# A head's groups of small matmuls moved earlier in the steps, to the places where attention's small matmuls stand

## The reference

```python
h = rmsnorm(x, w_norm_pre)
q_a, k_a, v_a, z_a, q_r, f_r, i_r, z_r = split(h @ w_in)
# attention: 8 heads of 64, 2 key heads, chunks of 64, a window of 2 chunks
s = einsum('bclhgd,bcmhd->bchglm', qc, kb) * scale
p = softmax(concat([s, sink]))[..., :-1]
o_a = einsum('bchglm,bcmhd->bclhgd', p, vb) * silu(z_a)
# recurrence: 4 heads of 128
f = lb + (1 - lb) * sigmoid(f_r);  G = cumsum(log(f)) in a chunk
A = causal(einsum('bclhk,bcmhk->bchlm', q*exp(G), k*exp(-G)))
o_intra = A @ v;  U = k_to_end^T @ v;  state = decay * state + U
o_inter = (q*exp(G)) @ state_before
o_r = rmsnorm(o_intra + o_inter) * silu(z_r)
x = x + rmsnorm(concat([o_a, o_r]) @ w_out, w_norm_post)
```

## Time and profile before

| | |
|---|---|
| median of 3 runs | 920.6 us (919.56 to 921.97) |
| the profiled execution's own time | 921.76 us |
| its span, first to last instruction | 920.0 us |
| TensorE matmuls busy | 904.5 us, 98% of the span |
| VectorE busy | 537.3 us, 58% |
| ScalarE busy | 426.4 us, 46% |
| GpSimd busy | 176.8 us, 19% |
| large matmuls (L424 and L433), count | 3 x 832 and 3 x 256 |

### The profile page before, as it was taken

One profiled execution on the slowest core, in us unless ns is written; L12 is line 12 of the kernel. 1 busy time (PEld: TensorE's weight loads), 2 busy tenths in 40 slices (PEclk: granted clock), 3 DMA queues, 4 the chain that ended last, 5 costly groups with the idle time before them and its releaser, 6 DMA issues.

```text
span 920.0 us, 12100 instructions
## 1 busy us (share of the span) xinstructions
PE 904.5 (98%) x4504; PEld 745.2 (81%) x4504; DVE 537.3 (58%) x959; ACT 426.4 (46%) x818; POOL 176.8 (19%) x138
## 2 busy tenths in 40 slices
PE   7998999999999999999999999999999999999997
PEld 6786878878888787888888878888888888788886
DVE  6758887784654765664254567555525366744523
ACT  7655366664444444454234534464423453444322
POOL 1001222520200203342020112243101011203102
PEclk9999999999999999999999999999999999999999
DMA  8785565738967543443785652354378553244463
GB/s 303 234 307 172 202 201 162 278 138 344 399 212 295 191 161 112 163 164 134 270 301 206 229 183 95 138 180 162 129 281 321 184 181 127 103 138 175 146 230 137
DMA packets 52636, 186.02 MB, mean 202 GB/s; under 512 B 5857, under 2 KB 6113, under 8 KB 52577
## 3 DMA queue, kind: packets, MB, share of 16 engines
q1 hardware_dynamic: 49840, 178.29, 54.2%
q10 hardware_dynamic: 2736, 6.95, 1.9%
HBM read 141.18 MB, written 44.04 MB: 201 GB/s over the span
## 4 chain that ended last, share of the span: by engine, by line
PE 87%; DVE 5%; ACT 4%; issue 2%; POOL 1%; DMA 1%; SPq 0%; DVEq 0%; ACTq 0%
PE bank L424 54%; PE bank L433 19%; PE bank L448 3%; PE bank L464 2%; PE bank L458 1%; PE bank L485 1%; PE bank L499 1%; PE bank L489 1%; PE bank L497 1%; PE bank L478 1%; DMA x_in<-in_x 1%; ACT w_hi L624 1%; PE bank L473 1%; DVE w_lo L825 1%; DVE f_c L1044 0%
## 5 line engine op out<-in xcount | busy, mean ns | idle before, releaser
L424 PE MATMUL bank<-h_hi,w_hi 128*128 128x512 f32 x832 | 331.4, 399 | 2.2 <-issue 1.1
L424 PE MATMUL bank<-h_hi,w_lo 128*128 128x512 f32 x832 | 329.5, 396 | 0.0
L424 PE MATMUL bank<-h_lo,w_hi 128*128 128x512 f32 x832 | 326.8, 393 | 0.0
L424 PEld LDWEIGHTS bank<-h_hi,w_hi 128*128 128x128 f32 x832 | 156.8, 188 | 47.8 <-issue 15.2
L424 PEld LDWEIGHTS bank<-h_lo,w_hi 128*128 128x128 f32 x832 | 157.0, 189 | 31.7 <-issue 0.2
L424 PEld LDWEIGHTS bank<-h_hi,w_lo 128*128 128x128 f32 x832 | 157.2, 189 | 30.2 <-issue 0.7
L1086 POOL TENSOR_TENSOR probs<-probs,s_stats 128x512 f32<-128x512 f32 x32 | 37.1, 1158 | 407.2 <-DVE s_stats L956 407.2
L433 PE MATMUL bank<-w_lo,mix_hi 128*128 128x512 f32 x256 | 100.0, 390 | 0.0
L433 PE MATMUL bank<-w_hi,mix_lo 128*128 128x512 f32 x256 | 99.9, 390 | 0.0
L433 PE MATMUL bank<-w_hi,mix_hi 128*128 128x512 f32 x256 | 99.6, 389 | 0.0
L825 DVE TENSOR_TENSOR w_lo<-w_raw,w_hi 128x1024 fp32r<-128x1024 f32 x37 | 49.7, 1352 | 23.3 <-ACT w_hi L624 23.2
(11 more groups left out here) (139 smaller groups left out, 1283.7 us busy)
## 6 DMA issues: line engine op xcount, KB each, us to landing
w_hi<-kept_hi SPq DMA_DIRECT2D x96, 512.0 KB, 3.7
w_lo<-kept_lo SPq DMA_DIRECT2D x96, 512.0 KB, 4.6
w_raw<-in_weights SPq DMA_DIRECT2D x40, 512.0 KB, 5.4
kept_hi<-w_hi SPq DMA_DIRECT2D x34, 512.0 KB, 5.9
kept_lo<-w_lo SPq DMA_DIRECT2D x34, 512.0 KB, 7.0
x_in<-in_x_rows SPq DMA_DIRECT2D x8, 1024.0 KB, 7.5
x_in<-in_x SPq DMA_DIRECT2D x15, 512.0 KB, 6.6
out<-q_gate ACTq DMA_DIRECT2D x9, 512.0 KB, 8.1
```

What stands on the lines that cost most here:

```text
L424: mm = pe.matmul(acc(w)[:, :], stationary[:, s, k, :], moving[:, k, :], start=(m == 0), stop=(m == 3 * KT - 1), skip_group_check=True)
```

## The change

Three numbers in `between` are other: the head's turns stand before large matmul 12 of their step instead of 18, its products before 4 instead of 8, its outputs before 4 instead of 10.

```diff
                 for h in range(HEADS):
-                    if w == gate(h) and m == 18:
+                    if w == gate(h) and m == 12:
                         head_turn(t, h)
-                    if w == gate(h) + 1 and m == 8:
+                    if w == gate(h) + 1 and m == 4:
                         head_products(t, h)
-                    if w == gate(h) + 2 and m == 10:
+                    if w == gate(h) + 2 and m == 4:
                         head_out(t, h)
                     if w == gate(h) + 3 and m == 18:
                         head_sum(t, h)
```

## The result

| | before | changed |
|---|---|---|
| median | 921.17 us (6 runs) | 924.45 us (6 runs, 922.50 to 926.78) |
| ratio, 95% interval | | 1.0036 (1.0022 to 1.0050) |
| span of the profiled execution | 920.0 us | 924.9 us |

What follows compares the result with a forecast made beforehand. TensorE bounds the kernel, its matmuls filling 904.5 of 920.0 us. Terms 0 (standing together) + 1.7 (tile 0) + 0.0 (head 3 later) + 0.1 (head 2's outputs) = +1.8 us on a 920.6 median: 922.4 us, range 920.4 to 924.4.

Steps and rivals of the forecast that it cites:

- Standing together: 16 moved groups that come to stand beside an attention group: no cheaper than apart, 0 us saved.
- Head 1's and head 2's turns, tile 0: L478 would wait for `v_r`, losing 0.65 us at head 1 and 0.73 us at head 2.
- Head 3's turns, tile 0: TensorE late by 1.37 us plus any later arrival of `v_r`, whatever was lost before: 1.7 us when tile 0 ends.
- the shift of `v_r`: Head 3, tile 0: how much later `v_r` comes, taken as +0.3 us, between about -0.5 and +1.38.
- The outputs of head 2: Tiles 1 and 2: wait for the last state of 0 to 0.1 us, taken as 0.1 for both together.
- the relief: Head 2, tile 1: earlier turns let GpSimd's L1109 and L1116 end near 395.8 and 397.1, states ready near 399.95.
- A wait before L497: Sign that the prediction is wrong; it expected L497 in tile 1 without a wait, or one under 0.1 us.
- the bounds: Limits on TensorE's lateness when tile 0 ends: 0.9 and 2.75 us.
- A: Head 2's and head 3's inputs stay: 2.75 us in tile 0, 0.74 in tiles 1 and 2 each; 924.8 us; chance 0.15.
- B: Groups standing together save 1.4 us against 1.8 lost: +0.4, 921.0 us; chance 0.1.
- C: Tile 0 catches up: `v_r` of head 3 comes 0.5 us earlier, tile 0 costs 0.9, 921.5 us; chance 0.2.
- D: Both B and C, and attention's wait for ScalarE shrinks by at most 0.7 us: -1.2, 919.4 us; chance 0.05.

Runs made afterwards that it cites:

- Experiment 4: Kernel before, with the turns, products and outputs at the changed places in tiles 1 to 3 only; ratio to the kernel before 0.9992.
- experiment 8: Changed kernel, with the squares of the next tile's x at other steps, taking one GpSimd add from ahead of L1116; ratio to the kernel before 1.0043.
- experiment 5: Changed kernel, with head 3's turns in tile 0 back before large matmul 18; ratio to the kernel before 1.0012.
- experiment 1: Kernel before, with only the heads' turns moved, before large matmul 12 instead of 18 in all tiles; ratio to the kernel before 1.0040.
- experiment 6: Kernel before, with only head 3's turns in tile 0 moved, before large matmul 12 instead of 18; ratio to the kernel before 1.0018.
- experiment 10: Kernel before, with only head 3's turns in tile 0 moved later, before large matmul 23 instead of 18; ratio to the kernel before 0.9984.
- experiment 11: Kernel before, with head 3's turns before 23 and the first chunk's weighted values before 21 instead of 12, both in tile 0; ratio 0.9980.
- experiment 12: Kernel before, with head 3's turns before 23 and the first three chunks' weighted values before 21, in tile 0; ratio 0.9964, 917.96 us.
- experiment 7: Changed kernel, with ScalarE's and GpSimd's split of attention's outputs (L772, L1109) one step earlier; ratio to the kernel before 1.0095.

## Why the prediction was wrong, point by point

*Standing together: 0.* Right. Experiment 4 has 12 merged groups, and over them its trace keeps the distances of before to 0.05 us. In the changed kernel turns and weighted values together cost 1.66 us in tiles 1 to 3, which is 0.88 + 0.78. TensorEngine Tiling (Array Packing), Key Properties, in the Trainium skill says that it is the change of mode that drains; the trace agrees.

*Head 1's and head 2's turns, tile 0: 0.65 and 0.73.* Right: 0.68 and 0.80 by the lateness. But attention's wait in step 16 gave 0.3 back ahead of them, and the wait before L506 0.55 behind them; neither had a term.

*Head 3's turns, tile 0.* The rule held: TensorE is late by what its place moved plus the shift of `v_r` (1.37 + 1.41 = 2.78 us against 2.74 in the changed kernel, 1.37 + 0.53 = 1.90 against 1.87 in experiment 8). The step that failed is the next one, where I took the shift as +0.3 us, "since part of that chain waits for GpSimd and not for TensorE". It was 1.4 to 1.5 us (1.41 in the changed kernel, 1.46 in experiment 5), a little over the upper end of what I had written down: tile 0 cost 2.7 us of waits, not 1.7. The reading behind it was carried over from tile 1. There ScalarE's L759 had waited 2.45 us for the turns, so GpSimd's work came earlier. In tile 0 ScalarE waited 0.5 us there, and GpSimd did not come earlier: L1116 ended 0.35 us later, start-up taken out.

Followed along VectorE's rows, start-up taken out, the shift is 1.2 us at L890, the gate's first step, since TensorE was late, and 1.6 at L906, as L894 between them took 1.77 us instead of 1.33. In the kernel before L906 had been held too, and L915 behind it had waited 0.54 us for L1116; by that slack L915 came only 1.0 us later. But the first L920 now took 1.16 us instead of 0.66, so L978 and `v_r` came 1.4 us later. Experiment 8 tells what this place was worth: with L906 and the first L920 free, 0.53 us of shift was left. So the thought that a part of the lateness is lost in GpSimd's part of the chain was not empty; it failed because GpSimd's work stayed where it was and held VectorE again. The Trainium skill (SBUF — State Buffer, SBUF: two separate sides) has this lock, by which, for some of VectorE's instructions, the one of VectorE and GpSimd that comes second fully blocks until the other's instruction is over; L906's 1.32 us, which end with L1116, agree. I used it in tile 1, where it came out to 0.1 us, and did not work it out in tile 0.

*The outputs of head 2.* In tiles 1 and 2 right, with the relief. In tile 0 I had no term: L497 waited 1.01 us. A wait before L497 was one of the signs by which the prediction was to be known as wrong, and it came there. By itself it costs nothing (experiment 1 lacks it and loses as much), because what comes behind waits for VectorE's chain too and takes it in: `head_sum`'s wait before L506 goes, and that of head 3's turns is shorter. It shows the same late chain.

*The clock.* This term was missing altogether. Behind the 1.95 us wait at 73.98 the kernel before already had 3.4 us at the lower level in its trace, and I predicted a wait of 1.75 us and, in the bounds, one of up to 2.8, without asking what the clock does behind it. It cost about 1.65 us in the profiled execution. For the median there is an estimate from the times: at a mean clock of 0.998 or 0.999, 17 of 19 executions of the kernel before take 919.6 to 920.6 us, and the changed kernel's two at 0.999 take 922.5 and 922.8. That is +2.6 us, about the waits alone, and would have been within the range; the median has about 0.7 more. Two executions are few, so this split of the median is not shown as firmly as that of the trace.

*Rivals.* A (slower, 924.8) came nearest in size, and was right that `v_r` of head 3 shifts by all of TensorE's lateness in tile 0, but not in its other half: no output waited in tiles 1 and 2. Its size was in part luck, since the clock made up for that half. B, C and D did not happen, but for the 0.3 us of D at attention's second wait. I gave A 0.15; the rows for more were there, since L890 and L978 follow TensorE closely.

## What to carry to other kernels

A small group on the critical engine wants a place behind its input at which nobody yet waits for it, not the earliest: moved earlier past its input it turns into a wait (experiment 6, +1.3 us), and moved later behind it the wait goes (experiment 10, -1.15 us), unless the next group waits in its place (experiment 11). Engines that are fed by the late engine pass its lateness on to the next group's input. So work out each input's slack in the tile where it is smallest, and take nothing from a tile where the other engines idle over to one where they are busy. Before merging groups to save switches, add up the distances of the same groups apart and together in the trace: here 0.89 + 0.55 = 1.44.

## What the runs showed of the hardware that was not expected

A pause of TensorE of about 2 us costs more than itself, but not in every execution. The timeline of PE in the kernel before has one, which the prediction did not use; the row of the kernel before under experiment 12 shows the clock there:

```profile
73.98 0.91 PE L464 MATMUL bank<-probs_t,v_tok 128*64 128x256 f32 x4 [1.95 <-ACT probs_t L732]
```

Over the 14 profiles, by TensorE's pauses behind start-up:

| pause | times seen | with 3.4 us at half clock near its end |
|---|---|---|
| 1.0 to 1.8 us | 12 | 0 |
| 1.95 to 1.96 us (L464, first chunk) | 12 | 9 |
| 2.35 to 2.8 us (L478, head 3) | 6 | 5 |
| 3.4 us (L506, experiment 7) | 1 | 1 |

The drop began between 0.5 us before and 1.4 us behind the end of the pause. In experiment 1, where it began before, it cost 1.4 us; in the others it cost 1.6: eight large matmuls at 0.43 instead of 0.23 us. The times of a kernel's own runs (919.6 to 923.9 us before) go with it, but not by it alone: in the kernel before, ten executions at a mean clock of 0.999 have a median of 920.1 us, and 35 at 0.995 one of 922.0. It is also why experiment 12's trace gained more than its waits. Why four of the longer pauses had no drop behind them is left open; no experiment was made on it.
